# A six-row ring with all of w_out resident, in a fused decoder-step kernel

## The reference, cut to what matters

```
h   = rmsnorm(x); p = h @ w_in                       # 1024 -> 3072 columns
mix = concat[conv(p), rwkv7(p), stick_breaking(p)]   # 256 + 384 + 384 = 1024
x   = x + mix @ w_out                                # w_out: 1024 x 1024
h2  = rmsnorm(x)
q   = h2 @ w_query; s = q . sub_keys                 # 8 heads, 2 sides, 128 keys
e   = the 16 best of 128*128 experts per token and head; gate = softmax(their scores)
act = gelu(peer_u[e] . h2)                           # peer_u, peer_v: 16384 x 1024
x   = x + sum over heads and experts of gate * act * peer_v[e]
y   = rmsnorm(x)
```

## Time and profile before

| | us |
|---|---|
| median of 3 runs | 3461.32 (3460.79 to 3462.07) |
| the profiled execution | 3464.72 |
| its span, first to last instruction | 3462.9 |
| busy: PE, DVE, ACT, POOL | 2815.9, 2530.2, 1644.4, 1333.6 |
| mean granted TensorE clock | 0.884 |

### The profile page before, as it was taken

How to read it: one execution, slowest core, us unless ns; L and a number is a source line. 1 busy time by engine, 2 the same in 40 slices (tenths; PEclk the granted TensorE clock), 3 DMA queues, 4 the chain that set the end, 5 groups by cost and what they waited for, 6 DMA issues and landing times.

```text
span 3462.9 us, 53594 instructions
## 1 busy us (share of the span) xinstructions
PE 2815.9 (81%) x19302; PEld 1368.1 (40%) x19302; DVE 2530.2 (73%) x5894; ACT 1644.4 (47%) x4402; POOL 1333.6 (39%) x1199
## 2 busy tenths in 40 slices
PE   9999777788688778886788788888888798867667
PEld 5666464334244324432443344334433244323211
DVE  2587235878777977797778877887788777777775
ACT  2222122547444744475446653674467434444443
POOL 0000001444454445434533464345444545554443
PEclk9999898989879888988898889888989888888989
DMA  3124344999999999999999999999999999999998
GB/s 106 34 71 122 122 170 168 405 417 394 409 417 402 417 414 416 399 416 416 416 403 411 414 412 407 412 417 412 418 404 417 412 393 416 401 414 417 419 420 348
DMA packets 248379, 1237.87 MB, mean 357 GB/s; under 512 B 61793, under 2 KB 92433, under 8 KB 112561
## 3 DMA queue, kind: packets, MB, share of 16 engines
q0 software_dynamic: 160256, 1132.54, 79.8%
q1 hardware_dynamic: 87856, 101.90, 8.8%
HBM read 1210.82 MB, written 23.53 MB: 356 GB/s over the span
## 4 chain that ended last, share of the span: by engine, by line
DMA 35%; PE 18%; DVE 17%; ACT 8%; issue 5%; POOL 2%; SPq 0%; DVEq 0%; ACTq 0%; POOLq 0%
DMA uv_ring<-in_peer_uv,expert 35%; PE peer_y L2481 9%; DVE uv_ring L1773 7%; ACT L2006 2%; PE beside L2072 2%; POOL uv_ring L1340 2%; PE scan L2160 1%; PE peer_s L2035 1%; ACT diag L2009 1%; DVE same L1384 1%; DVE same L1386 1%; ACT gelu L2006 1%; DVE pick L1388 1%; PE peer_y L2477 1%; ACT L1794 1%
## 5 line engine op out<-in xcount | busy, mean ns | idle before, releaser
L1340 POOL DMA_INDIRECT uv_ring<-in_peer_uv,expert x1056 | 1181.3, 1119 | 1654.9 <-PE peer_y L2481 1301.4
L2481 PE MATMUL peer_y<-uv_ring,diag 64*64 64x512 f32 x8192 | 1249.3, 718 | 487.7 <-ACT diag L2009 442.1
L1773 DVE CUSTOM_DVE_ANT_0 uv_ring<-uv_ring,p_h 128x1024 f32<-128x1024 f32 x1056 | 1276.6, 1224 | 493.1 <-DMA uv_ring<-in_peer_uv,expert 484.6
L2006 ACT ACTIVATE gelu<-hidden 128x1 f32<-128x1 f32 x1056 | 211.9, 201 | 1222.0 <-DVE hidden L1773 1217.9
L2481 PEld LDWEIGHTS peer_y<-uv_ring,diag 64*64 64x64 f32 x8192 | 282.6, 150 | 1104.8 <-ACT diag L2009 824.2
L2009 ACT ACTIVATE diag<-diag,gelu 128x64 f32<-128x64 f32 (+1 forms) x1056 | 366.3, 347 | 34.8
L2035 PE MATMUL peer_s<-wk,p_h2t 128*128 128x256 f32 x1024 | 314.5, 435 | 4.3 <-DVE cand L1365 4.2
L597 PE MATMUL proj<-mix,w_in_tile 128*128 128x352 f32 x1008 | 301.3, 460 | 0.0
L2035 PEld LDWEIGHTS peer_s<-wk,p_h2t 128*128 128x128 f32 x1024 | 191.5, 207 | 260.4 <-issue 236.7
L1975 ACT ACTIVATE diag<-ident_halves,p_gate 128x64 f32<-128x64 f32 x1024 | 292.7, 333 | 1.1 <-PE peer_y L2481 1.1
L597 PEld LDWEIGHTS proj<-mix,w_in_tile 128*128 128x128 f32 x1008 | 190.9, 190 | 104.2
(11 more groups left out here) (448 smaller groups left out, 3642.3 us busy)
## 6 DMA issues: line engine op xcount, KB each, us to landing
uv_ring<-in_peer_uv,expert POOLq DMA_INDIRECT x1056
w_in_tile<-in_w_in SPq DMA_DIRECT2D x24, 512.0 KB, 3.3
w_out_rows<-in_w_out SPq DMA_DIRECT2D x24, 512.0 KB
uv_ring<-in_w_query SPq DMA_DIRECT2D x8, 1024.0 KB, 7.3
scan_in<-scratch_scan_in SPq DMA_DIRECT2D x15, 480.0 KB, 8.5
pages_ring<-scratch_k_tiles SPq DMA_DIRECT2D x36, 192.0 KB
pages_ring<-out_v_new SPq DMA_DIRECT2D x36, 192.0 KB, 8.3
p_x<-in_x_rows SPq DMA_DIRECT2D x9, 512.0 KB, 8.6
```

Of the source, the lines that this page charges most:

```text
L1340: pool.indirect_dma_start(out=uv_row(m), out_offset=None, in_=io["peer_uv"], in_offset=bass.IndirectOffsetOnAxis(ap=expert[:, t % 4, k:k + ...
L1773: nc.vector.tensor_tensor_reduce(out=u_row(m), in0=u_row(m), in1=h2[:, b % 2, :], scale=1.0, scalar=0.0, op0=ALU.mult, op1=ALU.add, accum_ ...
L2006: nc.scalar.activation(gel[:, g % 2, k:k + 1], hid[:, g % 2, k:k + 1], ACT.Gelu_apprx_tanh).then_inc(gelu_done, 1)
L2481: ins = nc.tensor.matmul(Y[r][rows[j], :], diag[rows[r], m % DIAGS, :], v_row(m, rows[r], slice(j * 512, (j + 1) * 512)), start=begin, sto ...
```

## The change

The ring has six rows (48 KB), `wo` has eight slabs (32 KB): the same 80 KB as before. All of `w_out` is loaded once, in two halves of four slabs, at the place of the two former loads. `weights`, its semaphore `streamed` and `CLOSED_IN` are gone: slabs are closed in the order 0 to 7, and PE's waits for attention and recurrent parts are made once, at slabs 5 and 2, instead of at each slab.

```diff
-RING = 7
+RING = 6
...
-    STREAMED, W_OUT = tuple(range(3)), DC - 3 + 1
-    CLOSED_IN = (0, 5, 6, 1, 7, 3, 2, 4)
+    W_OUT = DC
...
-        rows_at_first = sb.ring[:, 1 + SLOTS:, :].rearrange("p r (c d) -> p (r c) d", d=D)[:, 0:len(STREAMED), :]
-        wo_of = lambda b, c: wo[:, c - len(STREAMED) + 1, :] if c not in STREAMED else wo[:, 0, :] if b else rows_at_first[:, c, :]
+        wo_of = lambda b, c: wo[:, c, :]
...
-            def weights(b, n):
-
-                c = STREAMED[n]
-                if n:
-                    sp.wait_ge(wo_used, b * DC + CLOSED_IN.index(STREAMED[n - 1]) + 1)
-                elif b > 1:
-                    sp.wait_ge(wo_used, (b - 1) * DC + CLOSED_IN.index(STREAMED[-1]) + 1)
-                sp.dma_start(wo[:, 0, :], io["w_out"][:, c, :]).then_inc(streamed, 16)
...
-            sp.dma_start(rows_at_first, io["w_out"][:, 0:len(STREAMED), :]).then_inc(wo_in[0], 16)
-            sp.dma_start(wo[:, 1:, :], io["w_out"][:, len(STREAMED):, :]).then_inc(wo_in[1], 16)
+            for n in range(2):
+                half = slice(n * DC // 2, (n + 1) * DC // 2)
+                sp.dma_start(wo[:, half, :], io["w_out"][:, half, :]).then_inc(wo_in[n], 16)
...
-                    weights(b + 1, 0)
...
-                    for n in range(1, len(STREAMED)):
-                        weights(b + 1, n)
...
-            def close_y(b, n):
-
-                c = CLOSED_IN[n] if b else n
-                if n == 0:
+            def close_y(b, c):
+
+                if c == 0:
...
-                if c >= DC - PA:
+                if c == DC - PA:
...
-                if CT <= c < CT + PR:
+                if c == CT:
...
-                if b == 0 and c in (0, len(STREAMED)):
+                if b == 0 and c in (0, DC // 2):
                     pe.wait_ge(wo_in[c != 0], 16)
-                if b and c in STREAMED:
-                    pe.wait_ge(streamed, 16 * ((b - 1) * len(STREAMED) + c + 1))
```

More of the change, by code:

```diff
@@ L1106, in peer @@
         mix_in, x_in, wo_in, wo_used = sem("mix_in"), [sem(f"x_in{n}") for n in range(2)], [sem(f"wo_in{n}") for n in range(2)], sem("wo_used")
-        streamed = sem("w_out_streamed")
         rows_set, page_in, k_used, v_used = sem("page_rows_set"), [sem(f"page_in{n}") for n in range(PAGES)], sem("k_used"), sem("v_used")
@@ L2038, in score @@
                     ins.then_inc(score_done, 1)
-            def close_y(b, n):
-                c = CLOSED_IN[n] if b else n
-                if n == 0:
+            def close_y(b, c):
+                if c == 0:
                     if b == 0:
-                        for k in range(2):
-                            pe.wait_ge(sb.wk_kept[k], PH * 2)
+                        for n in range(2):
+                            pe.wait_ge(sb.wk_kept[n], PH * 2)
                     if 0 < b < ATTENDED:
@@ L2066, in close_y @@
                 left = mixb[:, c, :] if c < CT else recurrent[:, c - CT, :] if c < CT + PR else att[:, c - (CT + PR), :]
-                if b == 0 and c in (0, len(STREAMED)):
+                if b == 0 and c in (0, DC // 2):
                     pe.wait_ge(wo_in[c != 0], 16)
-                if b and c in STREAMED:
-                    pe.wait_ge(streamed, 16 * ((b - 1) * len(STREAMED) + c + 1))
-                for k in range(2):
-                    ins = nc.tensor.matmul(CB(b)[k][:, :], left[:, :], wo_of(b, c)[:, k * 512:(k + 1) * 512], start=n == 0, stop=n == DC - 1)
+                for n in range(2):
+                    ins = nc.tensor.matmul(CB(b)[n][:, :], left[:, :], wo_of(b, c)[:, n * 512:(n + 1) * 512], start=c == 0, stop=c == DC - 1)
                 ins.then_inc(wo_used, 1)
```

## The result

The changed kernel takes 3494.4 us (3487.8 to 3501.7) against 3461.1 before: a ratio of 1.0098, 95% interval 1.0084 to 1.0111, slower by 33 us. The forecast was 3509, slower by 48. Single executions of the changed kernel lie 14 us apart, those of the kernel before 3 us.

The account below looks back on a forecast made before the run. The prediction took DMA to bound the loop from 600 to 3400 us. Span 3462.9 - 31 (streamed loads) + 79 (ring) = 3511, on the median 3461.3 + 48 = 3509 us; range 3442 to 3578, the forecast's own 3470 to 3551.

Parts of the forecast that it names:

- The limit: Main loop, 600 to 3400 us: the DMA engines are busy 1.01 of the time at 411 GB/s, no compute engine full.
- The forecast of the rate (400): Main loop of the changed kernel: mean DMA rate falls below 405 GB/s, to 400, from 411.
- The streamed loads, 31 us: Hardware DMA queue: dropping 24 loads of 512 KB of `w_out`, 12.6 MB, saves 31 us, range 30 to 38.
- No wait of PE, no effect of the order: PE's `w_out_rows` matmuls: no wait for streamed slabs to win back; new slab order counted 0, bound 0 to 5 us.
- The ring, 79 us: Gaps between POOL's ring issues: six rows cost 37 us at 15 gaps over 8 us, 41 at 33 of 6 to 8.
- The bounds of the ring: Loss from one ring row less: low 20 us (16 gaps at 1.25), high 159 us (120 for 48 gaps, 39 for 63 shorter).
- The lower end of 3442: Whole kernel time: bottom of the stated range 3442 to 3578 us, said to leave out a lower third of one rival.
- (B): Ring: six rows are cover enough, DMA stays full through gaps, 0 to 20 us lost, 3430 to 3450 us; chance 0.14.
- The account closes: Loop today: two costly gaps per period, 4.6 us, over eight periods give 37 us, close to 40 us from the rates.
- (C): Whole kernel: ring loss of 24 to 38 us nearly cancels the saved loads, 3454 to 3468 us; chance 0.08.
- (E): Main loop: streamed loads filled otherwise empty DMA moments, removal returns little, ring loss alone, 3540 us; chance 0.09.
- (D): TensorE: dry moments lower its clock, slots free later, gaps lengthen; 82 us more, up to 3591 us; chance 0.14.

Follow-up runs that it names:

- both single-part runs: Two runs against the kernel before: six ring rows with the streamed loads kept, ratio 1.0197; seven rows with the 24 streamed loads left out, ratio 0.9929.

## Why the prediction was right, and where it was not

**The limit** was read rightly. DMA bounds the loop: its share is 1.00 to 1.01 in all kernels but the one with five rows, and taking bytes away shortens the time by their price. The forecast of the rate (400) was met by 402.

**The streamed loads, 31 us.** Measured 25 us with seven rows and 34 with six, on either side of the term. The packets agree: between 600 and 3400 us the hardware queue's take 118 us of the 16 engines before and 88 with seven rows and no loads, 30 us less. The first load being free and the neglect of everything else SP does are within that. The 35 us that the prediction works out from the 358 GB/s of the Trainium skill (page "DMA: Bandwidth & Descriptors", section "Bandwidth") would also have been within the scatter. That section adds that each core gets about this rate when both cores of an HBM domain stream, and here one core runs alone; so the 411 of the earlier trace rows does not contradict it, and the figure was the wrong one for this case.

**No wait of PE, no effect of the order.** The wait for `att_block` (9.8 us in the earlier trace rows) is gone from the changed kernel, whose matmuls of L2055 wait for issue alone; the run with the old order shows no difference. The term of 0 stands.

```profile
L2055 PE MATMUL beside<-w_out_rows,att_block x96: 592/592/697, 750.1 to 3248.4; 128*128 128x512 f32 x96
...
  issue: 37.2, 134
```

**The ring, 79 us: the mis-sized term.** It measures 58 to 68 us. The place was right (behind long gaps, quiet stretches hardly touched), the price too high. The sum had 79 us behind the 48 gaps over 6 us; there the loss rose by 51 us (36 to 87), and behind the shorter ones, left out of the sum, by 9 (only 1 in the kernel with six rows and the loads). In the windows of block 2 above, six rows add 7.2 us over six gaps (11.8 against 4.6), 1.2 us a gap, where the sum put 1.25 on a gap of 6 to 8 us and 2.5 on a longer one. That eight blocks at 7.2 give just the 58 us that were measured is chance: by block the loss grew by 6, 8, 9, 11, 11, 12, 2 and 2 us.

Two things were wrong in the price. First, it went by the length of a gap and took every gap over 8 us as past the dry point. What the traces show to matter as much is how many rows were outstanding (issued, and not yet being read by DVE) when the gap began. Before, the 7 gaps over 8 us that began with all seven rows outstanding lost 1.8 us together, the 8 that began with six lost 19. With six rows the 10 that began full lost 15, 1.5 us each, and the 12 others 39, 3.2 each. So the row less cost 1.2 us at the first kind and 0.8 at the second, where the sum had 2.5. (Among the gaps of 6 to 8 us the number outstanding makes no such difference.) Second, the gaps were counted in the kernel before and held fixed, and this went the other way: the changed kernel has 22 gaps over 8 us, 36 of 6 to 8 and 97 of 4.5 to 6, against 15, 33 and 63. Had the counts held, the rise behind the gaps over 6 us would have been about 31 us and not 51 (15 times 1.0 and 33 times 0.5, the growth of the mean loss per gap of each class). The price was too high and the count too low, and that the two partly cancel is luck.

Not all of the loss is idle engines. From before to the changed kernel the rate falls by 2.1% (410.9 to 402.2 GB/s by the packets), the busy share only by 1.0% (1.007 to 0.996). The other half is that the gathers' packets (most are of 8 KB) take longer behind the long gaps: there 1 MB of them takes 2.48 us of the 16 engines before and 2.55 in the changed kernel, elsewhere 2.41 to 2.43. The prediction knew dry moments only; what lengthens the packets is open.

**The range.** The bounds of the ring, 20 and 159 us, give 3450 to 3589; the forecast's own range, 3470 to 3551, is that of 40 to 120 us, and no step leads from one to the other. The 3494 lies in both. The lower end of 3442 also leaves out three fifths of (B)'s 3430 to 3450, not a third.

**"The account closes"** was the weak sentence. 37 us from two gaps a period and 40 us from the rates agreed, and I took both for a price that more rows would save. The place was right, as the table shows (36 of 41 us behind gaps over 6 us), though the blocks are less alike than the sum had them: they lose 4 to 10 us, the last one nothing. But a further row returned 6 to 10 us, because much of the loss lies behind long gaps that begin with the ring not full, and with eight rows more of POOL's gaps are long. It did not hurt the forecast, because the sum used the *added* cost of a row and not this total.

**The rivals.** (B), six rows are enough, is out: the ring alone costs 68 us where it needed under 31. (C) would have needed 24 to 38 us. (E), loads in dry moments, is out by both single-part runs. (D), compounding through TensorE's clock, asked for a fall of the clock and more value matmuls at 1.2 GHz. The mean clock of the profiled executions went from 0.884 to 0.880, and single executions lie at 0.880 to 0.887 against 0.878 to 0.892 for the kernel before. All value matmuls together went from 1249.3 to 1263.4 us:

```profile
L2464 PE MATMUL peer_y<-uv_ring,diag 64*64 64x512 f32 x8192 | 1263.4, 723 | 488.0 <-ACT diag L1995 394.2
```

The kernel with the shorter ring alone, 68 us slower, has 1253.3 us and a clock of 0.888 in its profile. So (D) is no second mechanism at the scale of the ring's loss, though a low clock goes together with the length of one gap, as shown above. With five rows it begins to show: a value matmul takes 746 ns instead of 723, and the clock is 0.84 in the loop. By the Trainium skill (page "TensorE: Matmul & The Clock Gate", section "HAM oscillation"), waits for DMA between short bursts bring the clock down; the five-row run agrees in direction, but how much of its 201 us is the clock's was not tried.

On (B)'s rule, 2.0 us plus the bytes over 436 GB/s by the Trainium skill (page "DMA: Bandwidth & Descriptors", section "Anatomy of one DMA"), which is 4.4 us for 1 MB: the shortest time from an issue to its read is 5.7, 5.6 and 5.3 us with seven, six and five rows, and it takes in the issue itself and DVE's start, so no run here shows the 4.4 by itself. The rule is for one transfer; what set the depth here were bursts.

## What to carry to other kernels

When DMA is full, the worth of a buffer is not its mean occupancy but what is left of it at the end of the longest gap between issues: list the gaps, note for each how many slots were outstanding when it began, and take the shortest time from issue to read as what a slot needs. Here the added cost of one slot less was about half of its transfer time a gap (58 to 68 us over 48 gaps at 2.5 us a slot), and it grew steeply with the next one (201 us), while an eighth slot brought 6 to 10 us. What is lost behind one gap is not what its removal returns: of 19 us with six rows 12 came back in the time, of 13 us with seven only 3. Bytes removed from a full DMA queue come back at their price over the rate, so 12.6 MB traded for one ring row is a sum that can be done beforehand.

## What was not expected of the hardware

- With eight rows the DMA engines are busy 1.01 of the loop and still move 413 GB/s, where quiet stretches of the kernel before move 417 to 419 at 1.01 to 1.02. A share of 1.00 or 1.01 does not tell a loss of 1 to 2% from none; the rate does.
- Runs with six rows scatter more: 14 us between four executions of the changed kernel and 25 us between six of the one with the old order, against 8 us between 23 executions of the kernel before. Seven rows without the loads scatter by 13 us between five and eight rows by 3 us between four, so it is not the ring's depth alone; the cause stays open.
- With five rows the share falls to 0.95 at 376 GB/s, though in a quiet stretch by the numbers of the earlier trace rows a slot's round of 12.4 us still leaves 8.3 us where 5.7 are needed.
